# Expert SwiGLU of a two-layer decoder trunk: expert weights as plain fp32 in four 32-column tiles instead of split in two fp32r parts, with more weight buffers and an earlier router

## What is computed

```
def moe_ffn(h, w_router, wg, wu, wd):
    hf = h.reshape(b * s, d)                                  # 256 x 1024
    logits = (hf @ w_router).astype(jnp.float32)              # 256 x 8
    topv, topi = lax.top_k(logits, TOP_K)
    wts = jax.nn.softmax(topv, axis=-1)
    gate = jnp.sum(jax.nn.one_hot(topi, N_EXPERTS) * wts[..., None], axis=1)
    for e in range(N_EXPERTS):
        out = out + gate[:, e:e + 1] * swiglu(hf, wg[e], wu[e], wd[e])   # 1024 -> 3584 -> 1024
```

## Time and profile before

| | us |
|---|---|
| median of 3 runs | 1637.74 (1635.88 to 1637.77) |
| the profiled execution, its own time | 1636.9 |
| its span | 1635.1 |
| TensorE matmul busy | 1595.0 (98% of the span) |
| weight loads of TensorE busy | 1291.2 (79%) |
| VectorE busy | 975.3 (60%) |
| ScalarE busy | 800.0 (49%) |
| HBM read | 475.61 MB, mean 292 GB/s |

### The profile page before, as it was taken

How to read it: one execution, slowest core, us unless ns; L and a number is a source line. 1 busy time by engine, 2 the same in 40 slices (tenths; PEclk the granted TensorE clock), 3 DMA queues, 4 the chain that set the end, 5 groups by cost and what they waited for, 6 DMA issues and landing times. The chain is left out here.

```text
span 1635.1 us, 21947 instructions
## 1 busy us (share of the span) xinstructions
PE 1595.0 (98%) x9231; PEld 1291.2 (79%) x9231; DVE 975.3 (60%) x772; ACT 800.0 (49%) x699; POOL 48.1 (3%) x111
## 2 busy tenths in 40 slices
PE   8999999999999999989999999999999999998997
PEld 7999898999989998978873478888843788535885
DVE  4555646554455656459871088888810788204985
ACT  5444454443444435447750177777600677104774
POOL 1000000000000001033000000000000000000000
PEclk9999999999999999999999999999999999999999
DMA  9555544465565545388989999999989999999990
GB/s 342 181 181 180 201 141 155 141 207 187 167 208 199 171 165 198 125 309 319 356 331 399 403 409 405 407 409 390 370 349 403 409 409 403 409 403 409 409 400 39
DMA packets 164102, 478.09 MB, mean 292 GB/s; under 512 B 8516, under 2 KB 13732, under 8 KB 164004
## 3 DMA queue, kind: packets, MB, share of 16 engines
q1 hardware_dynamic: 164004, 476.69, 78.1%
HBM read 475.61 MB, written 1.05 MB: 292 GB/s over the span
## 5 line engine op out<-in xcount | busy, mean ns | idle before, releaser
L573 ACT ACTIVATE whi<-raw 128x2048 fp32r<-128x2048 f32 (+1 forms) x206 | 389.5, 1891 | 256.7 <-PE ps L1388 108.0
L946 DVE TENSOR_TENSOR wlo<-raw,whi 128x2048 fp32r<-128x2048 f32 (+1 forms) x116 | 259.0, 2236 | 210.8 <-ACT whi L573 210.7
L1713 PE MATMUL ps<-whi,a_hi 128*128 128x512 f32 x1120 | 352.5, 396 | 9.7 <-DVE a_hi L951 9.7
L951 DVE TENSOR_TENSOR wlo<-raw_more,whi 128x2048 fp32r<-128x2048 f32 x120 | 274.3, 2291 | 42.1 <-ACT whi L573 41.8
L1388 PE MATMUL ps<-a_hi,whi 128*128 128x256 f32 x992 | 281.4, 284 | 0.0
L1388 PE MATMUL ps<-a_hi,wlo 128*128 128x256 f32 x992 | 280.7, 283 | 0.0
L1388 PE MATMUL ps<-a_lo,whi 128*128 128x256 f32 x992 | 280.7, 283 | 0.0
L573 ACT ACTIVATE whi<-raw_more 128x2048 fp32r<-128x2048 f32 x120 | 229.4, 1916 | 50.7 <-PE ps L1742 28.6
L1713 PEld LDWEIGHTS ps<-whi,a_hi 128*128 128x128 f32 x1120 | 209.5, 190 | 56.1 <-DVE wlo L951 9.6
L951 DVE TENSOR_TENSOR wlo<-raw,whi 128x2048 fp32r<-128x2048 f32 x90 | 204.1, 2287 | 77.0 <-ACT whi L573 76.9
L1713 PE MATMUL ps<-wlo,a_hi 128*128 128x512 f32 x560 | 220.5, 394 | 0.0
(11 more groups left out here) (248 smaller groups left out, 1999.6 us busy)
## 6 DMA issues: line engine op xcount, KB each, us to landing
raw_more<-in_w_e_up SPq DMA_DIRECT2D x80, 1024.0 KB, 16.3
raw_more<-in_w_e_gate SPq DMA_DIRECT2D x64, 1024.0 KB, 18.0
raw<-in_w_e_down SPq DMA_DIRECT2D x64, 1024.0 KB, 16.1
raw<-in_w_e_gate SPq DMA_DIRECT2D x48, 1024.0 KB, 18.1
raw_more<-in_w_e_down SPq DMA_DIRECT2D x48, 1024.0 KB, 14.9
raw<-in_w_in SPq DMA_DIRECT2D x32, 1024.0 KB, 5.5
raw<-in_w_e_up SPq DMA_DIRECT2D x32, 1024.0 KB, 17.7
raw<-in_w_xk SPq DMA_DIRECT2D x8, 1024.0 KB, 5.3
```

Source lines behind the costliest of these rows:

```text
L573: return act.activation(dst, src, ACT.Copy, scale=scale)
L946: dve.tensor_tensor(wlo[n % SPL][:, 0:size], raw[n % RAW][:, 0:size], whi[n % SPL][:, 0:size].bitcast(F32), ALU.subtract).then_inc(s["lo_r ...
L951: return dve.tensor_tensor(dst, src, hi.bitcast(F32), ALU.subtract)
L1713: ins = pe.matmul(bank(b0 + c), (heh, hel)[xi][:, kt, :], w[wi][:, k, c * C:(c + 1) * C], start=kt == 0 and n == 0, stop=kt == KD - 1 and ...
```

## The change

All eight visits now take the raw fp32 unit. The slots are the stationary operand in blocks of 32 columns, and four column tiles of the array work side by side on four quarters of the unit's columns. A heavy visit has room for 96 tokens (three blocks, `SG` = 3), a light one for 64 (two blocks); the light visits are now 1, 4 and 7, so that the last visit is light. Per unit there are 24 matmuls of 256 columns in a heavy visit and 16 in a light one (the last group: 48 and 32 of 128 columns). `expert_hi`, `expert_lo`, `act_hi`, `act_lo`, `gathered_lo` are gone. The freed split buffers and others make 21 weight buffers; `slot_wait` always waits for TensorE. The results of a visit lie in PSUM by quarters and are moved to `y_slots` in 32-row pieces (8 to 12 small copies, half on ScalarE, half on VectorE) before the split in `yh`, `yl`. Scatter 2 and 3 stand earlier. The router takes its logits from x without the norm (the order of the logits of a token does not depend on it, and the softmax's difference is multiplied with `rstd` after); x is transposed straight from `x_res`, its first half inside the last dense chunk; the normalized rows for the gather are made by VectorE (`h_rows`). Overflow takes up to 16 further visits instead of 8.

```
-MR = 14
+MR = 21
+SG = 3
+CAP = 32 * SG
-RANK_OF_VISIT = (7, 0, 3, 4, 1, 5, 2, 6)
-LIGHT = (1, 4, 6)
-STEADY = 7
+RANK_OF_VISIT = (7, 0, 3, 4, 1, 5, 6, 2)
+LIGHT = (1, 4, 7)
+STEADY = 6
...
+    SPLITS = [place_of[f"{w}{(U0 - SPL + i) % SPL}"] for i in range(SPL) for w in ("whi", "wlo")]
+    slots = [moe_top, place_of["b_hi"], place_of["b_lo"], sc + 24576, place_of["kT"], place_of["v_tok"], sc + 16384] + [
+        place_of[f"raw{(U0 + i) % RAW}"] for i in range(RAW)] + SPLITS + [place_of["a_lo"], sc]
...
                 def slot_wait(i, v):
-                    pv, pi = (v, i - MR) if i >= MR else (v - 1, i + BODY - MR)
-                    if isinstance(pv, int) and pv in LIGHT:
-                        sp.wait_ge(s["unit_used"], pv * BODY + U0 + pi + 1)
-                    else:
-                        sp.wait_ge(s["lo_ready"], split_units(pv, pi + 1))
+                    n = i - MR
+                    sp.wait_ge(s["unit_used"], every(v, BODY, U0 + n + 1))
...
                 for i in range(MR):
+                    if i == 1:
                         sp.wait_ge(s["unit_used"], mix_start[-1])
+                    elif i == 4:
                         sp.wait_ge(s["o_done"], NH * DEPTH)
+                    elif 7 <= i < 7 + RAW:
+                        sp.wait_ge(s["lo_ready"], U0 - RAW + i - 7 + 1)
+                    elif 7 + RAW <= i < 7 + RAW + 2 * SPL:
+                        sp.wait_ge(s["unit_used"], U0 - SPL + (i - 7 - RAW) // 2 + 1)
+                    elif i == MR - 1:
                         sp.wait_ge(s["hg_ready"], NT)
...
-                def gate_up(i, v):
...
-                        for c in range(n_c):
-                            for n, (wi, xi) in enumerate(PASSES):
-                                ins = pe.matmul(bank(b0 + c), (heh, hel)[xi][:, kt, :], w[wi][:, k, c * C:(c + 1) * C],
-                                                start=kt == 0 and n == 0, stop=kt == KD - 1 and n == 2)
+                def gate_up(i, v, n_groups):
...
+                        for h in range(n_groups):
+                            for q in range(4):
+                                ins = pe.matmul(o[q * QP:(q + 1) * QP, h * n:(h + 1) * n],
+                                                he[:, kt, h * QP:(h + 1) * QP], w[:, k, q * n:(q + 1) * n],
+                                                start=kt == 0 and h * n % C == 0, stop=kt == KD - 1, skip_group_check=True)
...
+                def y_hi(v, n_groups):
+                    used = n_groups * QP
+                    act.wait_ge(s["unit_used"], every(v, BODY, U0))
+                    act.wait_ge(s["t_done"], every(v, NG4, 0))
+                    for q in range(2):
+                        for g in range(n_groups):
+                            ins = copy(y_rows(g, q), y_piece(g, q))
+                    ins.then_inc(s["yact_done"], 1)
+                    for c, done in enumerate(("yact_done", "ydve_done")):
+                        act.wait_ge(s[done], every(v, 1, 1))
+                        copy(yh[0:used, c * C:(c + 1) * C], y32[0:used, c * C:(c + 1) * C], gc[0:used, 0:1]).then_inc(s["yhi_ready"], 1)
...
-                        chunk_n(2, XA, already)
-                        keep_clock(18)
-                        transposes(xn, 0, KD // 2)
...
+                        chunk_n(2, XA, already, early=lambda: transposes_x(0, 2, first_half))
...
+                for k in range(KD // 2):
+                    logits(k)
+                transposes_x(2, 4, second_half)
+                keep_clock(8)
+                for k in range(KD // 2, KD):
+                    ins = logits(k)
```

More of the change, by code:

```diff
@@ L202, in trunk @@
[L202 to L211, removed]
@@ L235, in trunk @@
[L235 to L240, removed]
+        region[0] += (n + 63) // 64 * 64
@@ new lines, in trunk @@
+    iota = moe("iota_slots", [P, P], F32, fixed)
+    tri = moe("strict_upper", [P, P], F32, fixed)
+    ones = moe("ones", [P, P], F32, fixed)
+    wr2 = moe("w_rout_parts", [P, KD, 2 * NE], F32R, fixed)
+    rev = moe("rev_index", [P, NT, NE], F32, small)
+    rt = [moe(f"route{i}", [P, NT, NE], F32, small) for i in range(6)]
+    rc = [moe(f"route_c{i}", [P, NT], F32, small) for i in range(9)]
+    lgt = moe("logits", [P, NT, NE], F32, small)
+    pos = moe("rank", [P, NT, NE], F32, small)
+    gate = moe("gate", [P, NT, NE], F32, small)
@@ new lines, in trunk @@
+    posv = moe("rank_of_visit", [P, NT, COLS], F32, small)
+    gatev = moe("gate_of_visit", [P, NT, COLS], F32, small)
+    above, within = [moe(f"rank_{n}", [P, NT, NE], F32, small) for n in ("above", "within")]
+    first = moe("first_spilled", [P, NT, 1], F32, small)
+    table = [moe(f"table{i}", [P, NE, NE], F32, tables) for i in range(3)]
+    row = [moe(f"row{i}", [P, NE], F32, tables) for i in range(7)]
+    e_iota = moe("expert_iota", [P, NE], F32, tables)
+    rank_of = moe("rank_of_visit_no", [P, NE], F32, tables)
@@ L442, in _ @@
+                with sp.If(last > NE - 1):
+                    for r in range(ROUNDS):
+                        with sp.Fori(0, NE) as e:
+                            load(e, e + (NE - 1 + r * NE))
+                load(sp.value_load(eid[0:1, NE - 1:NE], min_val=0, max_val=NE - 1), last)
+                sp.wait_ge(s["unit_used"], every(last, BODY, U0 + MR + 1))
+                sp.dma_start(gfin[:], a["g_final"].rearrange("(a d) -> a d", a=1).broadcast_to([P, D])
                              ).then_inc(s["gfin_loaded"], 16)
@@ L518, in _ @@
                 less, at_visit, prod = table
-                count, key, cap, eidf, over, any_over = row[:6]
+                count, key, cap, eidf, over, any_over, none_over = row
                 pool.wait_ge(s["hg_ready"], NT)
@@ new lines, in visit @@
+                def visit(v, n_groups=SG, after_groups=SG, more=True):
+                    y_lo(v, after_groups)
+                    for n in range(4):
+                        add_piece(n, v)
+                    act_rows(0, v, n_groups)
+                    slot_rows(v)
+                    if more:
+                        dve.wait_ge(s["table_ready"], 1)
+                        select(bass.ds(every(v, 1, 1), 1), posv)
+                    for g in range(1, NG4):
+                        act_rows(g, v, n_groups)
+                    if more:
+                        gathered(every(v, 1, 1))
@@ L1615, in _ @@
[L1615 to L1622 removed]
+                keep_clock(20)
                 pe.wait_ge(s["hot_ready"], 1)
```

691 lines of the change are left out of this document (293 added, 398 removed).

## The result

The changed kernel takes 1618.71 us (median of 4 runs, 1616.56 to 1619.56), the kernel before 1636.81 beside it: ratio 0.9889, 95% interval 0.9876 to 0.9903. It is 1.1% faster, where 3.1% was forecast: 18 of 51 us. The profiled execution took 1619.56, its span is 1617.8.

The account below looks back on a forecast made before the run. TensorE bounds the dense part, TensorE and DMA lie close in the expert part; afterwards TensorE is the limit. First visit at 723.4, five heavy visits of 120.1, three light of 83.0, and the tail give about 1586 us; range 1566 to 1655.

Parts of the forecast that it names:

- its own case: The prediction's main case, no matmul step over 0.219 us: 1570 to 1605 us, chance 0.66.
- Four tiles: Expert matmuls: four tiles run side by side, a step of four taking 0.216 us, or 0.109 at half length.
- rivals A: Expert matmuls: four tiles run no more than two at once, 2349 us; chance 0.08, three at once included.
- B: Expert matmuls: a fixed cost per record that four tiles do not hide; 1605 to 1634 us had chance 0.09.
- Interruptions and visits: Scatters, transposes and gather on TensorE add 11.1 us a heavy visit, 10.3 a light one: visits of 120.1 and 83.0.
- Short steps: Half-length steps of group 3 in each visit: issue could limit them, at most 10 us, left to the range.
- the prediction's own signs of being wrong: Steps over 0.229 us, idle time "issue" between matmuls, or waits for `h_slots` or `y_lo` at a visit's start.
- Rival D: Instruction fetches in the visits each hold TensorE 1.1 us: 134 us, 1720; chance 0.10 shared with B beyond its decision point.
- Buffers and transfers: Expert weight loads: with 21 buffers the lead never reaches zero, TensorE waits for no weight; DMA could end at 1543.
- Router and tail: Before and after the visits: first visit at 723.4, 7.2 us earlier; tail 14.4 us, about 1.3 longer.
- Rival C: Expert visits: the DMA stays the limit, or TensorE's interruptions are shorter than read; floor 1562 us, chance 0.05.

Follow-up runs that it names:

- e2: Changed kernel with every expert load after the first 21 bringing only a quarter of each row, TensorE's program the same: 1585.81 us.
- e4: Changed kernel with 14 weight buffers in place of 21: 1622.01 us.
- e5: Changed kernel with the last group's gate and up units using 64-column tiles for the first 64 slots, all before the 32-column ones: 1590.43 us.
- e7: Changed kernel with every expert load after the first 21 bringing three quarters of each row: 1600.83 us.
- f2: Changed kernel with SyncE letting no more than four expert loads be under way at once: 1619.15 us.

## Why the prediction was wrong, and what of it held

The forecast was 1586 us, with 1570 to 1605 for its own case; 1618.7 was measured. One term failed, that of the short steps in the last group of columns, which need instructions faster than they come; the other terms of the sum held.

**Four tiles (rivals A and B).** Right: 0.216 and 0.109 us a step of four, to the nanosecond; no record pays for its issue. The time did fall in the band that was B's (1605 to 1634, chance 0.09), but not for B's reason.

**Interruptions and visits.** Right when nothing starves TensorE: 118.2 to 120.0 and 84.6 us in e2, whose light window holds a heavy visit's last units (1.6 us more than the 83.0 forecast) and the next heavy one a light visit's. All eight visits take 845.5 us there, where 845.6 were forecast.

**Short steps.** This is the step that failed: "Those short steps could be limited by issue (124 ns): 672 steps, at most 10 us; I leave that to the range." The sum had nothing for them. The term was mis-sized in value and in cause. It measured 33 us, the distance to e2: 23.4 us of standstill in the 128-column units and the transposes between them (21.8 + 1.6 on "issue"), 5 us at 1.2 GHz behind them (three times 1.7), the rest in a start 0.8 us later and in delays of about half a microsecond a visit. Idle time on "issue" between matmuls stood among the prediction's own signs of being wrong. The limit isn't how fast a pair is handed out, but how fast instructions arrive.

**Rival D.** I had the right queue, and the right time of a fetch (1.1 us, 1.07 in the trace), but spread the fetches over the whole span: "122 fetches, one every 7 us", and "a fetch can run 7 us ahead". In the last group one is needed every 3.5 us, and comes every 6.2. In the long stretches fetching costs nearly nothing, so D's price (134 us, each fetch holding TensorE for 1.1) was wrong too. And I never asked what a fetch shares the DMA with.

**Buffers and transfers.** The conclusion was right, that TensorE waits for no weight. The reason given, 21 buffers, was not needed: with 14 it waits 0.5 us in all (e4). And the DMA isn't throttled to 367 GB/s in heavy visits, since each light visit empties the buffers that the next heavy ones refill at 406 (visit 2 above). That is why it was full at just the place where instructions were wanted.

**Router and tail.** Right within a microsecond: first visit 724.3 for 723.4, tail 14.8 for 14.4.

**Rival C** falls: e5 with quarter loads is no faster.

What stays open: by which mechanism a full DMA delays the start of a packet of the instruction queue (a turn among queues or the memory behind them), and from what share on; e7 doesn't settle that. Why a pause costs the clock in one visit and not in another is open too.

## What to carry to other kernels

Count instructions per microsecond, stretch by stretch, not over the span: here 37 a microsecond went through beside 400 GB/s of weights, and 73 did not. Where a tile gets short, use fewer and wider tiles for it, and keep each form together: e5 takes 28 us off the changed kernel and ends 2.9% under the one before. To find what transfers cost an engine, cut their bytes and leave the program alone.

## What the runs showed of the hardware

A 16 KB fetch of instructions comes every 6.2 us when TensorE wants more beside a full DMA (408 GB/s), every 3.5 to 3.7 when the DMA is a third full (95 GB/s). TensorE goes on 1.2 to 1.5 us after it has landed. A pause of 2.5 us in a dense stream lowered the clock to 1.2 GHz in three visits of four; a pause of 2.00 us (visit 4) didn't. But f2 had the same four pauses of 2.5 us and lost the clock behind one, and it lost it in visit 0 behind a pause of 1.98 us, so the length of the pause doesn't decide alone:

```profile
824.86 2.61 PE L1622 MATMUL ps<-slot,h_slots 128*32 128x128 f32 x67 [1.98 <-issue]
...
826.00:830.00 4.00, 4.00 (x67) 3.74 (x59) 0.55 (x1) 0.00 (x0) 0.00 (x0) 0.57 0.42 116
```

A change between 64- and 32-column tiles and back costs 0.29 us.
